# Attention gate of a hybrid decoder: scaled by ScalarE, turned in 32 x 32 blocks by VectorE, put in place by transfers, in place of TensorE's transposes

## What is computed

```python
z = x @ w_in;  q, k, v, g_attn, hq, hf, hi, g_hg = split(z)
q, k = rope(q), rope(k)
attn = sink_window_attend(q, k, v)               # 8 heads of 64, 2 key heads, window 128
attn = rmsnorm(attn, attn_g) * silu(g_attn)      # the gate of the attention branch
o_hg = rmsnorm(hgrn2(hq, hf, hi, lb, state), hg_g) * silu(g_hg)
mix  = concat(attn, o_hg) @ w_out
h    = layernorm(alpha * x + mix, ln_g, ln_b)
y    = h + sigmoid(h @ w_pg) * (p @ w_pp)
```

## Time and profile before

| | us |
|---|---|
| median of three runs | 2550.71 |
| the three runs | 2550.71, 2557.65, 2549.84 |
| the profiled execution's own time | 2546.3 |
| its span | 2544.5 |
| TensorE busy (matmul) | 2493.5 |
| VectorE busy | 1705.2 |
| ScalarE busy | 1113.5 |
| GpSimd busy | 1172.3 |

### The profile page before, as it was taken

The page is one execution under the profiler, slowest core; times in us unless marked ns, Lnnn a source line. Parts: engine busy times, 40 slices in busy tenths (PEclk is TensorE's granted clock), DMA queues, the critical chain, the costliest instruction groups (busy, mean ns, idle before and its releaser), DMA issues. The chain is left out here.

```text
span 2544.5 us, 55195 instructions
## 1 busy us (share of the span) xinstructions
PE 2493.5 (98%) x20706; PEld 2044.3 (80%) x20706; DVE 1705.2 (67%) x3230; ACT 1113.5 (44%) x2542; POOL 1172.3 (46%) x1119
## 2 busy tenths in 40 slices
PE   8999989999999999999999999899999999999998
PEld 6788868888888788888888788688888887887887
DVE  5777777777676676654557777776777676866343
ACT  4455465555555510133334454555555554112322
POOL 2234315555556611496322443165555555116863
PEclk9999999999999999999999999999999999999999
DMA  5445552011110488765734555510111005877532
GB/s 182 154 172 185 187 186 70 27 43 43 44 38 25 175 288 293 273 216 172 264 123 154 186 179 178 190 35 31 43 43 51 31 33 195 313 270 257 170 135 91
DMA packets 176099, 365.44 MB, mean 144 GB/s; under 512 B 19104, under 2 KB 98464, under 8 KB 170272
## 3 DMA queue, kind: packets, MB, share of 16 engines
q1 hardware_dynamic: 175504, 363.11, 41.6%
q10 hardware_dynamic: 432, 0.08, 0.0%
HBM read 227.14 MB, written 137.89 MB: 143 GB/s over the span
## 5 line engine op out<-in xcount | busy, mean ns | idle before, releaser
L1947 PE MATMUL r_Z<-w_rec_parts,w_rec_xh 128*128 128x512 f32 x1920 | 610.3, 399 | 1.8 <-DVE r_kT L1768 0.9
L1947 PEld LDWEIGHTS r_Z<-w_rec_parts,w_rec_xh 128*128 128x128 f32 x1920 | 347.7, 188 | 71.9 <-issue 3.5
L1947 PE MATMUL r_Z<-w_rec_parts,w_rec_xl 128*128 128x512 f32 x960 | 375.7, 391 | 0.0
L124 PE MATMUL a_Z<-w_attn_high,w_attn_xh 128*128 128x512 f32 (+1 forms) x816 | 302.3, 370 | 11.6 <-DVE w_attn_low L211 9.7
L124 PE MATMUL a_Z<-w_attn_low,w_attn_xh 128*128 128x512 f32 (+1 forms) x816 | 290.6, 356 | 0.0
L124 PE MATMUL a_Z<-w_attn_high,w_attn_xl 128*128 128x512 f32 (+1 forms) x816 | 290.3, 356 | 0.0
L1649 ACT ACTIVATE r_E<-r_E 128x512 f32<-128x512 f32 x230 | 145.3, 632 | 294.6 <-DVE r_E L1805 292.1
L1540 POOL TENSOR_TENSOR r_qE<-r_qT,r_E 128x256 f32<-128x256 f32 x230 | 185.1, 805 | 190.6 <-ACT r_E L1649 115.4
L1947 PEld LDWEIGHTS r_Z<-w_rec_parts,w_rec_xl 128*128 128x128 f32 x960 | 180.2, 188 | 39.7
L1540 POOL TENSOR_TENSOR r_kE<-r_kT,r_E 128x256 f32<-128x256 f32 x230 | 201.2, 875 | 0.0
L124 PEld LDWEIGHTS a_Z<-w_attn_high,w_attn_xh 128*128 128x128 f32 x816 | 154.8, 190 | 39.9 <-issue 19.3
(11 more groups left out here) (338 smaller groups left out, 6409.3 us busy)
## 6 DMA issues: line engine op xcount, KB each, us to landing
dram_h_rows<-o_hb SPq DMA_DIRECT2D x34, 512.0 KB, 4.1
o_raw<-dram_hT SPq DMA_DIRECT2D x34, 512.0 KB, 4.3
o_hb<-dram_h_rows SPq DMA_DIRECT2D x34, 512.0 KB, 3.8
dram_y_all<-o_hb SPq DMA_DIRECT2D x34, 512.0 KB, 4.1
w_attn_xraw<-dram_xT SPq DMA_DIRECT2D x33, 512.0 KB, 5.7
w_rec_slot<-dram_w_in SPq DMA_DIRECT2D x16, 1024.0 KB, 8.2
o_mraw<-dram_mixT SPq DMA_DIRECT2D x32, 512.0 KB, 5.6
dram_hT<-o_hT SPq DMA_DIRECT2D x128, 128.0 KB, 2.6
```

What stands on the lines that cost most here:

```text
L124: mm = pe.matmul(out, a[:, c, :], b[:, c, :], start=(first and c == chunks[0] and a is xh and b is wh), stop=(last and c == chunks[-1] and ...
L1947: mm = pe.matmul(banks[what], x[:, c, :], w[:, cols[what]], start=(c == 0 and x is xh[k] and w is wh[c]), stop=(c == KC - 1 and x is xl[k]))
```

## The change

For tiles 1 to 14 of each layer the scaled gate is no longer turned by TensorE. `scale_gate` moves from VectorE to ScalarE, behind `split_high` and ahead of `high_part` and `exps`. `turn_gate`, new on VectorE ahead of `row_max`, transposes the 4 x 4 x 4 blocks of 32 x 32 within their partitions into `th`. SyncE then stores `th` to DRAM in four transfers, each of which takes 32 partitions to their places, and loads the turned gate back into `attn` (`store_gate`, `load_gate_turned`). `gated` reads it from there (SBUF) and stands behind `unfold`. `gate_tanh` of tile n+1 waits for the load of tile n-1, since it writes `th` too; `values` waits for the mean square and no longer for `gated`. Tiles 0, 15 and 16 are turned by TensorE as before. In the output phase only names of semaphores change (`hT_st` and `h_in` become `turned_st` and `turned_in`); those hunks and the counts are left out below.

```diff
@@ -529,6 +529,10 @@
 
         own, before = slice(P, 2 * P), slice(0, P)
 
+        def by_transfer(n):
+
+            return not isinstance(n, int) or 1 <= n <= NT - 3
+
         part = [weights.beside[n][:, :] for n in ("part0", "part1")] + [kcT[:, :, :].rearrange("p b d -> p (b d)")]
         part_high, part_low = (weights.beside[n] for n in ("part_high", "part_low"))
         part_in = S["part_in0"], S["part_in1"], S["part_in2"]
@@ -599,6 +603,24 @@
                         of, to = slice(HD * s, HD * s + HD), slice(HD * e, HD * e + HD)
                         sp.dma_start(dram["mixT"][n - 1, to, 2 * s:2 * s + 2, :], mixT[k][of, e::2, :])\
                             .then_inc((S["mix_st0"], S["mix_st1"])[k].sem, 16)
+
+            def gate_home(n):
+                return dram["hT"][layer, n][:, 0:AW]
+
+            def store_gate(j, k):
+
+                n = 2 * j + k
+                sp.wait_ge(*S["turned"].at(n))
+                for i in range(4):
+                    sp.dma_start(gate_home(n).rearrange("(q r) (i x) -> i r q x", q=4, i=4)[i],
+                                 th[32 * i:32 * i + 32, :].rearrange("r (q x) -> r q x", q=4))                        .then_inc((S["turned_st0"], S["turned_st1"])[k].sem, 16)
+
+            def load_gate_turned(j, k):
+
+                n = 2 * j + k
+                sp.wait_ge(*(S["turned_st0"], S["turned_st1"])[k].at(64 * (j + k)))
+                sp.wait_ge(*S["uT_out"].at(n))
+                sp.dma_start(attn[:, :], gate_home(n)).then_inc(S["turned_in"].sem, 16)
 
             if layer == 0:
                 load_x(0, 0)
@@ -649,13 +671,19 @@
             load_part(2)
             load_gate(0)
             load_x(2, 1)
+            store_gate(0, 1)
+            load_gate_turned(0, 1)
             for j in range(1, PAIRS - 1):
                 c = 4 * (j - 1)
+                store_gate(j, 0)
+                load_gate_turned(j, 0)
                 exchange_part(c)
                 store_mix(j - 1, 1)
                 load_x(j + 2, 0)
                 exchange_part(c + 1)
                 store_mix(j, 0)
+                store_gate(j, 1)
+                load_gate_turned(j, 1)
                 exchange_part(c + 2)
                 if j + 2 < PAIRS:
                     load_x(j + 2, 1)
@@ -665,6 +693,8 @@
             lead.load_x(sp, 0)
             following.load(sp, dram, layer, 6, 7)
             store_mix(PAIRS - 2, 1)
+            store_gate(PAIRS - 1, 0)
+            load_gate_turned(PAIRS - 1, 0)
             sp.wait_ge(*S["z_g"].at(NT))
             following.load(sp, dram, layer, 0, 4)
             sp.wait_ge(*lead.S["x_split"].at(1))
@@ -772,6 +802,8 @@
                 n = 2 * j + k
                 act.wait_ge(*S["z_g"].at(n + 1))
                 wait(act, S["gate_done"], n)
+                if not isinstance(n, int) or n > 2:
+                    act.wait_ge(*S["turned_in"].at(16 * (n - 2)))
                 act.activation(th[:, :], Zg, ACT.Tanh, scale=0.5).then_inc(S["tanh_done"].sem, 1)
 
             def copy_v(j, k):
@@ -820,6 +852,19 @@
                                        scale=SCALE, accum_out=rowsum[:, h:h + 1])
                     heads = slice(4 * s, 4 * s + 4)
                     act.activation(sinke[:, heads], sinkd[:, heads], ACT.Exp).then_inc(S["exp_done"].sem, 1)
+
+            def scale_gate(j, k):
+
+                n = 2 * j + k
+                act.wait_ge(*S["rstd_done"].at(n + 1))
+                act.wait_ge(*S["gate_done"].at(n + 1))
+                if isinstance(n, int) and n == 1:
+                    act.wait_ge(*S["gT_ps"].at(1))
+                else:
+                    act.wait_ge(*S["turned"].at(n - 1))
+                act.activation(u[:, :].rearrange("p (i s d) -> p s i d", s=KV, d=HD),
+                               gate[k][:, :].rearrange("p (s i d) -> p s i d", s=KV, d=HD), ACT.Copy, scale=rstd[:, 0:1])\
+                    .then_inc(S["scaled"].sem, 1)
 
             def copy_attnT(j, k):
                 n = 2 * j + k
@@ -896,18 +941,22 @@
             j = 1
             copy_qkT(j, 0)
             split_high(j + 1, 0)
+            scale_gate(j - 1, 1)
             rest(j, 0)
             with act.Fori(2, PAIRS) as j:
                 copy_qkT(j - 1, 1)
                 split_high(j, 1)
+                scale_gate(j - 1, 0)
                 high_part(j - 2, 0)
                 rest(j - 1, 1, (j - 2, 1))
                 copy_qkT(j, 0)
                 split_high(j + 1, 0)
+                scale_gate(j - 1, 1)
                 high_part(j - 2, 2)
                 rest(j, 0, (j - 2, 3))
             copy_qkT(PAIRS - 1, 1)
             lead.split_high(act, 0)
+            scale_gate(PAIRS - 1, 0)
             exps(PAIRS - 1, 1)
             following.round(act, lead.S, layer, 6)
             copy_v(PAIRS, 0)
@@ -1029,14 +1078,29 @@
                 n = 2 * j + k
                 dve.wait_ge(*S["rstd_done"].at(n + 1))
                 dve.wait_ge(*S["gate_done"].at(n + 1))
-                wait(dve, S["gT_ps"], n)
+                if n == NT - 1:
+                    dve.wait_ge(*S["gT_ps"].at(2))
                 dve.tensor_scalar(u[:, :].rearrange("p (i s d) -> p s i d", s=KV, d=HD),
                                   gate[k][:, :].rearrange("p (s i d) -> p s i d", s=KV, d=HD), rstd[:, 0:1], None,
                                   ALU.mult).then_inc(S["scaled"].sem, 1)
 
+            def turn_gate(j, k):
+
+                n = 2 * j + k
+                dve.wait_ge(*S["scaled"].at(n + 1))
+                dve.transpose(th[:, :].rearrange("p (q i t) -> p q i t", q=4, i=4),
+                              u[:, :].rearrange("p (i q t) -> p q i t", q=4, i=4)).then_inc(S["turned"].sem, 1)
+
             def gated(j, k):
                 n = 2 * j + k
-                dve.wait_ge(*S["gT_ps"].at(n + 1))
+                if by_transfer(n):
+                    dve.wait_ge(*S["turned_in"].at(16 * n))
+                    wait(dve, S["attnT_done"], n)
+                    wait(dve, (S["mix_st0"], S["mix_st1"])[k], 64 * j)
+                    dve.tensor_tensor(in_tokens(mixT[k][:, :, :]), in_tokens(attnT[:, :, :]),
+                                      attn[:, :].rearrange("p (i c t) -> p c i t", i=4, c=4), ALU.mult)                        .then_inc(S["uT_out"].sem, 1)
+                    return
+                dve.wait_ge(*S["gT_ps"].at(2 if n == NT - 2 else 3))
                 wait(dve, S["attnT_done"], n)
                 wait(dve, (S["mix_st0"], S["mix_st1"])[k], 64 * j)
                 dve.tensor_tensor(mixT[k][:, :, :].rearrange("p j t -> p (j t)"),
@@ -1114,14 +1178,14 @@
 
             def step(j, k, *chunks):
                 sum_squares(j - 1 + k, 1 - k)
+                turn_gate(j - 1 + k, 1 - k)
                 row_max(j, k)
-                scale_gate(j - 1 + k, 1 - k)
                 for c in chunks[0:1]:
                     low_part(c, 2 * (1 - k))
                 divide(j, k)
                 rope(j + k, 1 - k)
+                unfold(j, k)
                 gated(j - 1 + k, 1 - k)
-                unfold(j, k)
                 gates(j + k, 1 - k)
                 for c in chunks[1:2]:
                     low_part(c, 1 + (1 - k))
@@ -1237,7 +1301,10 @@
                 n = 2 * j + k
                 wait(pe, S["unfolded"], KV * n)
                 pe.wait_ge(*S["v_moved"].at(n + 1))
-                wait(pe, S["uT_out"], n)
+                if isinstance(n, int) and n in (1, NT - 1):
+                    pe.wait_ge(*S["uT_out"].at(n))
+                else:
+                    pe.wait_ge(*S["ms_done"].at(n))
                 for r in (0, 64):
                     for s in range(KV):
                         d, queries = slice(HD * s, HD * s + HD), slice(r, r + 64)
@@ -1335,7 +1402,6 @@
                 sum_squares(j - 1 + k, 1 - k)
                 score(j, k)
                 z_q(j + k, 1 - k)
-                transpose_gate(j - 1 + k, 1 - k)
                 z_g(j + k, 1 - k, 0)
                 transpose_probs(j, k)
                 z_g(j + k, 1 - k, 1)
```

30 lines of the change are left out of this document (15 added, 15 removed).

## The result

The changed kernel takes 2580.84 us (median of 5 runs, 2573.62 to 2586.51); the kernel before took 2554.47 us in the runs beside it (2549.84 to 2562.88). The ratio is 1.0098, 95% interval 1.0067 to 1.0128: slower by 1%, some 25 us, where 2549.0 and no measurable difference were forecast, and outside the range. The profiled execution of the changed kernel took 2580.84 us, its span is 2579.0.

What follows compares the result with a forecast made beforehand. TensorE bounds the kernel, busy 2493.5 of 2544.5 us. Terms -11.4 + 1.0 - 0.7 + 3.6 + 5.8 = -1.7 take the profiled 2546.3 to 2544.6; with 4.4 to the median, 2549.0 us, range 2541.5 to 2560.0.

Steps and rivals of the forecast that it cites:

- What TensorE gains: Attention steps on TensorE: each group of four gate transposes gone saves 0.44 us, 26 groups, -11.4 us.
- The regular step: VectorE's fold 0.7 us later, unfolding at 162.15, TensorE wants it by about 162.35: some 0.2 us to spare, cost 0.
- the product's collisions: VectorE's moved gate product, reading two SBUF tiles, collides with GpSimd: 0 to 0.6 us a step over 8 steps, +1.0.
- Rival (b): Turn ahead of row maxima takes 1.2, not 0.7 us past the old fold; unfolding 0.3 late every step: +6.1; chance 0.16.
- Rival (d): VectorE's turn waits some 2.4 us for GpSimd's split of x; unfolding 1.4 late, 36 us more; chance 0.02.
- SyncE's queue: Steps 8, 10, 12: gate transfers delay the low part's store, ScalarE's high part 0 to 1.5 us late; 6 x 0.6 = +3.6.
- The step of tile 15: Gate scaled behind ScalarE's rounding: exponentials 3.15 us later, TensorE waits 2.6 to 3.2 longer; two layers, 2.9 each, +5.8.
- The base: Profiled execution 2546.3 us lies 4.4 below the median of three runs, 2550.7; so 2544.6 becomes 2549.0.
- two signs of being wrong: Recurrence or output phases change by over a microsecond; or tanh or the gate product waits for the turned gate's load.
- (a) cheap queue: Queue and end cost little: part stores land in time, tile 15 late by half; -9.2, 2541.5 us; chance 0.20.
- (c) full price: Steps 8, 10, 12 at 1.5 us each (9), product collisions 3, ends 6.4: +6.3, 2557.0 us; chance 0.13.

Runs made afterwards that it cites:

- experiment 5: The kernel before without TensorE's transposes of the gate for tiles 1 to 14, all else in place: 2549.86 us, ratio 0.9978.
- Experiment 4: The changed kernel without the gate's four stores and its load; scaling, turn and the product's place unchanged: 2558.34 us, ratio 1.0018 to the kernel before.
- experiment 6: The kernel before with the gate's four stores and a load nobody reads added at the change's place in SyncE's queue: 2584.86 us, ratio 1.0105.
- experiment 2: The changed kernel with tile 14's gate scaled on ScalarE ahead of the rounding of the recurrence's x: 2569.75 us, ratio 1.0066 to the kernel before.
- Experiment 9: The kernel before, unchanged, profiled once more: 2552.99 us, span 2551.2.
- experiment 7: The changed kernel with tile 14's scaling ahead of the rounding, weight loads ahead of gate stores, part stores ahead of the turned gate's load: 2555.66 us, ratio 1.0002.

## Why the prediction was wrong

**What TensorE gains: right, and a little small.** A group is worth 0.49 us in the changed kernel (19.30 to 18.81) and 0.50 in experiment 5; 0.44 were forecast. The price of 1.1 us a group, from the 275 ns that the Trainium skill ("TensorE: Matmul & The Clock Gate", Part 4) gives beside a bf16 transpose, is not borne out for these groups of four f32 transposes between projections.

**The regular step: the right mechanism, with no margin in place of 0.2 us.** In layer 0 the steps keep 18.81 us but for those behind tiles 6 and 7 (19.26 and 19.05). In layer 1 from tile 5 on those without a stall last 19.03 to 19.11, 0.2 to 0.3 us more, and 0.57 stands with VectorE's unfolding where 0.35 was. The forecast took this at nothing; with the product's collisions (+1.0 forecast) it is the 1.2 us that the 20 other steps fall short of. Rival (b), from 0.9 us in every step, did not come. Rival (d) neither: the turn takes 0.71 us under GpSimd's split (148.46 in 147.64 to 150.04 above), while the moved product, with two operands in SBUF, takes 1.14 at 159.99, under GpSimd's block of 159.29 to 160.58, where it took 0.68; it still takes 0.68 or 0.69 in the steps of tiles 3 to 5, where GpSimd does nothing at that time. That is the rule of the Trainium skill ("SBUF — State Buffer", Who interferes with whom) in both halves.

**SyncE's queue is the step that failed**: "they move from 190.17 to about 196.3 ... It is 0 to 1.5 us late ... I take 0.6". The place was right, the size was not: +3.6 were forecast; the ledger has +22.0, and with the 2.6 that TensorE's gain was to bring there, 24.6. That is 4.1 us a step where the bounds were 0 and 1.5. It failed in three ways.
- It followed the wrong transfer. It asked when the low part's *store* lands. ScalarE waits for the store, but also for the *load* of its input, which is issued behind both stores. In the changed kernel that load took 9.2 us, and it is what ScalarE's wait of 3.73 us in the step of tile 8 ends with. Experiment 4 shows that it had no slack even without more traffic.
- It read "late on the queue" as a shift of issue times, by absolute time, with 1.5 us at most added to the landing. The stores of the gate issued in 1.78 us and landed 1.8 after their issue, much faster than the 3.38 and 2.8 assumed; the part store even left earlier in absolute time (192.92 against 195.49). But TensorE was 3.3 us ahead by then and the weights' megabyte left 1 us later and not earlier (191.16 against 190.17), so all these transfers fell into one stretch. Of the 4.1 us by which the part's load lands later in its step, 0.7 are a later issue and 3.4 a longer landing (9.2 against 5.8); the low part's store, which the forecast did follow, took 8.5 us to land and not 4.2 to 5.7.
- It had no price for the clock. After the gap of 2.81 us TensorE ran at 0.50 for about three microseconds, and behind experiment 6's gap of 3.39 us in that step for longer. Beyond the gap these two steps are 1.6 and 2.8 us longer than a regular one (23.21 - 18.81 - 2.81 and 25.44 - 19.30 - 3.39), an estimate of what the clock took. The first profile of before shows 1.00 behind all of TensorE's waits in the attention phases and could not give it; but a wait of TensorE can cost more than its length here.

**The step of tile 15**: the delay of ScalarE's exponentials behind the rounding was forecast as 3.15 us, and it is 342.20 - (337.74 + 1.34) = 3.1. The wait of TensorE was sized at 2.9 from the unfolding; it is 4.5 at the transposes of the probabilities, which come earlier in TensorE's order, and the clock of 0.50 behind it costs more. So +10.9 came in place of +5.8, and experiment 2 gives 10.4 of it back with one moved line. Of the 10.9, 2.2 lie in the steps behind tile 15's value product; which wait makes those was not found.

**The base.** The 4.4 us between profile and median were added as they stood. Experiment 9 shows one thing that makes such a difference, the 11 us instruction. The forecast also named two signs of being wrong. One is there on its face: the stretch between the attention phases changed by 8.5 us, for the reason that experiment 9 gives and not by the change. The other isn't: in the changed kernel neither tanh nor the product waits for the load of the turned gate.

**The queue's rivals.** (a) cheap queue and (c) full price both lay far below what came: the bounds, 0 and 1.5 us a step, were taken from the wrong transfer and with too short a landing, so the range could not hold the time. With three moves, the weights ahead of the gate's stores, the part stores ahead of the load that waits and the scaling ahead of the rounding (experiment 7), the kernel is level with the one before: 1.0002. That is another kernel than the one forecast.

## What to carry to other kernels

A transfer that waits for another's landing holds up its whole queue. What it holds up is late itself, or leaves together with what follows and then takes longer to land, so look at both times. Put all that somebody waits for ahead of it, and price what it moves by the *last* transfer behind it, the load after the store included, in the time of the step and not by absolute time. Before trading TensorE work for transfers, take the work away alone (here 0.2%, since the next engine was 0.1 us behind) and add the transfers alone (1%): two runs warn of the trade. A moved instruction that stands behind an engine's longest wait should go ahead of it.
